# Two transformer blocks on one core: norm factors, gates, a weight's high part and the feed-forward squares put elsewhere

## The reference

```python
# block 1
h = rms_norm(x, g_mix_norm);  z = h @ w_in
y_a = mlstm_group(...)            # 4 heads, both directions:
#     h = rms_norm(h, g_out) per head;  return sigmoid(o) * h
y_b = mla_group(...)              # 4 heads of softmax attention
x = x + concatenate([y_a, y_b]) @ w_out
h = rms_norm(x, g_ffn_norm)
x = x + square(relu(h @ w_ff1)) @ w_ff2          # width 4096
# block 2
proj = rmsnorm(x, norm_mix_g) @ w_in
ry = retention(...)               # 4 heads
s = q k^T + bias;  p = softmax(s);  a = p[0] - lam * p[1];  dy = a @ v   # 4 heads, 4 query blocks
x = x + concatenate([ret_out, diff_out]) @ w_out
x = x + peer(rmsnorm(x, norm_ffn_g), ...)        # experts picked by product keys
return rmsnorm(x, final_norm_g)
# rms_norm(x) = x * rsqrt(mean(x*x) + 1e-6) * g
```

## Time and profile before

| | |
|---|---|
| median of 3 runs | 2349.71 us (2343.17, 2349.71, 2353.16) |
| the profiled execution's own time | 2352.68 us |
| its span | 2350.9 us |
| PE busy | 2288.5 us, 97% |
| DVE, POOL, ACT busy | 1347.7, 1178.3, 915.8 us |
| mean granted TensorE clock | 0.992 |

### The profile page before, as it was taken

One profiled execution on the slowest core, in us unless ns is written; L12 is line 12 of the kernel. 1 busy time (PEld: TensorE's weight loads), 2 busy tenths in 40 slices (PEclk: granted clock), 3 DMA queues, 4 the chain that ended last, 5 costly groups with the idle time before them and its releaser, 6 DMA issues.

```text
span 2350.9 us, 29628 instructions
## 1 busy us (share of the span) xinstructions
PE 2288.5 (97%) x11229; PEld 1143.2 (49%) x11429; DVE 1347.7 (57%) x2765; ACT 915.8 (39%) x1095; POOL 1178.3 (50%) x558
## 2 busy tenths in 40 slices
PE   8999999999999999999999999999999999999998
PEld 4556444444444564544566444444444444444443
DVE  3668474554425545898896555555555544555555
ACT  3233342333333443111687333344444334444432
POOL 1002346655543347410000676666666666888873
PEclk9999999999999999999999999999999999999999
DMA  6031358989752239834588886666666666776641
GB/s 220 0 108 37 142 168 247 259 238 262 226 156 72 72 126 261 223 117 157 206 323 311 286 244 201 197 197 192 192 194 189 193 170 176 200 203 172 173 113 45
DMA packets 404136, 427.16 MB, mean 182 GB/s; under 512 B 276258, under 2 KB 343078, under 8 KB 392500
## 3 DMA queue, kind: packets, MB, share of 16 engines
q1 hardware_dynamic: 397684, 414.05, 58.3%
q10 hardware_dynamic: 6336, 11.54, 1.3%
HBM read 286.06 MB, written 72.37 MB: 152 GB/s over the span
## 4 chain that ended last, share of the span: by engine, by line
PE 56%; DMA 2%; POOL 1%; ACT 1%; issue 1%; DVE 1%; SPq 1%; POOLq 0%; ACTq 0%; DVEq 0%
PE ps L1860 27%; PE ps L2168 23%; PE ps L2207 3%; DMA gate_matrix<-split 1%; PE ps L2184 1%; PE ps L2185 1%; DMA ring<-in_peer_v 1%; SPq L691 1%; PE ps L2133 1%; ACT split L1382 1%; POOL u_split L955 0%; POOL split L836 0%; PE ps L2073 0%; DMA arena<-u_split 0%; POOL u_split L841 0%
## 5 line engine op out<-in xcount | busy, mean ns | idle before, releaser
L1860 PE MATMUL ps<-split,arena 128*128 128x512 bf16 x3712 | 819.7, 380 | 5.8 <-DVE consts L2940 1.6
L1860 PEld LDWEIGHTS ps<-split,arena 128*128 128x128 bf16 x3792 | 371.1, 98 | 449.5 <-issue 4.3
L2168 PE MATMUL ps<-arena 128*128 128x512 bf16 x1886 | 415.7, 379 | 2.1 <-DMA arena<-u_split 0.3
L961 POOL TENSOR_TENSOR split<-ring,split 128x1024 bf16<-128x1024 f32 x140 | 299.3, 2146 | 76.4 <-ACT split L1417 76.4
L836 POOL TENSOR_TENSOR split<-ring,split 128x4096 bf16<-128x4096 f32 x26 | 207.2, 7971 | 197.1 <-ACT split L1189 194.7
L1860 PE MATMUL ps<-arena,split 128*128 128x512 bf16 x1316 | 296.8, 381 | 5.0 <-DVE arena L2640 2.0
L2168 PEld LDWEIGHTS ps<-arena 128*128 128x128 bf16 x1920 | 187.7, 98 | 227.2 <-DMA arena<-u_split 0.8
L955 POOL TENSOR_TENSOR u_split<-ring,u_split 128x1024 bf16<-128x1024 f32 x80 | 167.7, 2127 | 191.1 <-ACT u_split L1404 191.1
L947 POOL TENSOR_TENSOR split<-ring,split 128x1024 bf16<-128x1024 f32 x44 | 92.7, 2138 | 258.1 <-ACT split L1414 258.1
L1860 PEld LDWEIGHTS ps<-arena,split 128*128 128x128 bf16 x1344 | 142.9, 107 | 150.0 <-DVE arena L2640 6.1
L1417 ACT ACTIVATE split<-ring 128x1024 bf16<-128x1024 f32 x140 | 146.3, 1054 | 172.2 <-POOL ring L971 66.6
(11 more groups left out here) (357 smaller groups left out, 3125.1 us busy)
## 6 DMA issues: line engine op xcount, KB each, us to landing
ring<-in_peer_v SPq DMA_DIRECT2D x32, 2048.0 KB, 8.3
ring<-in_peer_u SPq DMA_DIRECT2D x20, 2048.0 KB, 12.0
ring<-in_w_ff SPq DMA_DIRECT2D x16, 2048.0 KB, 8.2
gate_matrix<-split SPq DMA_DIRECT2D x16, 2048.0 KB, 7.5
arena<-gate_matrix SPq DMA_DIRECT2D x32, 1024.0 KB, 6.8
arena<-in_peer_u SPq DMA_DIRECT2D x48, 512.0 KB, 4.8
turned_table<-u_split SPq DMA_DIRECT2D x48, 512.0 KB, 5.6
ring<-turned_table SPq DMA_DIRECT2D x12, 2048.0 KB, 9.1
```

The lines of the kernel that those rows point to most:

```text
L961: pool.tensor_tensor(part_place(i, 1), block, part_place(i, 0), ALU.subtract).then_inc(v_lo, 1)
L1860: mm = pe.matmul(dst, a(k), b(k), start=n == 0, stop=n == len(terms) - 1)
L2168: mm = pe.matmul(up_bank(j), a, b, start=n == 0, stop=n == len(terms) - 1)
```

## The change

It moves instructions of ACT, POOL and DVE, cuts two of ACT's into parts, and puts the feed-forward squares into PSUM, with the wait of PE that this needs. On POOL:

```diff
             mlstm_rms(0)
             mlstm_rms(1)
+            mlstm_rms(2)
             pool.wait_ge(w_hi, 1)
             ... (four first_low subtractions)
-            mlstm_rms(2)
             mlstm_rms(3)
@@
                 if s == 18:
                     inverse_rms(1, D, 33, 0)
+                    inverse_rms(1, D, 34, 1)
                 split_low(s, s % 4)
                 if s == 18:
-                    inverse_rms(1, D, 34, 1)
+                    inverse_rms(1, D, 35, 2)
                 for b in range(2):
                     pre_low(2 * (s - 3) + b, b)
-                    if s == 18 and b == 0:
-                        inverse_rms(1, D, 35, 2)
@@
             pre_late(SOON)
+            inverse_rms(1, D, 69, 0)
             split_low(27, 3)
-            inverse_rms(1, D, 69, 0)
             inverse_rms(1, D, 70, 1)
```

On ACT:

```diff
+                if t == 3:
+                    act.wait_ge(mm_out, 15)
+                    act.activation(o1[:, 0:3, :], o1[:, 0:3, :], ACT.Sigmoid).then_inc(o_sig, 1)
                 nope_rows(t)
             z_out(15)
             act.wait_ge(mm_out, 16)
-            act.activation(o1, o1, ACT.Sigmoid).then_inc(o_sig, 1)
+            act.activation(o1[:, 3, :], o1[:, 3, :], ACT.Sigmoid).then_inc(o_sig, 1)
@@
-            def out_high(c):
+            def out_high(c, part=slice(0, 4096), last=True):
                 act.wait_ge(ring_in[1 + c], arrived(1 + c, 1))
-                act.activation(split[:, c, 0, :], ring[:, 1 + c, :], ACT.Copy).then_inc(w_hi, 1)
+                step = act.activation(split[:, c, 0, part], ring[:, 1 + c, part], ACT.Copy)
+                if last:
+                    step.then_inc(w_hi, 1)
@@ for h in range(H):
                 attend_exp(4 * h + 1)
+                if h >= 2:
+                    out_high(0, slice(1024 * (2 * h - 3), 1024 * (2 * h - 2)), h == H - 1)
@@ (at the end of head h)
-                if h == 2:
-                    out_high(0)
+                if 1 <= h < H - 1:
+                    out_high(0, slice(2048 * (h - 1), 2048 * (h - 1) + 1024), False)
@@
             mix2_squares(0)
             split_high(18, 2, 5)
+            mix2_squares(1)
             pre_high(15, 0)
-            mix2_squares(1)
             pre_high(15, 1)
```

On PE and DVE (`hid` is gone from the memory plan, and DVE waits for `o_sig` 2 in place of 1):

```diff
                 for j in range(4):
-                    pe.wait_ge(ff_relu, 4 * g + max(j - 1, 0))
+                    pe.wait_ge(ff_lo, 4 * g + max(j - 1, 0))
@@ ff_square
-                    dve.tensor_tensor(hid[:, j % 2, :], relu[:, j % 2, :], relu[:, j % 2, :], ALU.mult).then_inc(ff_sq, 1)
+                    dve.scalar_tensor_tensor(bank(2 + j % 2), bank(2 + j % 2), 0.0, relu[:, j % 2, :], ALU.max, ALU.mult).then_inc(ff_sq, 1)
@@
-                    dve.tensor_tensor(hid_lo[:, par, j, :], hid[:, j % 2, :], hid_hi[:, par, j, :], ALU.subtract).then_inc(ff_lo, 1)
+                    dve.tensor_tensor(hid_lo[:, par, j, :], bank(2 + j % 2), hid_hi[:, par, j, :], ALU.subtract).then_inc(ff_lo, 1)
@@ for i in range(H * NT + 3):
+                if i == H * NT:
+                    mixed_probs(i - 1)
@@ (behind the copies)
                 if i == H * NT:
-                    mixed_probs(i - 1)
                     decayed_scores(0)
```

More of the change, by code:

```diff
@@ L242, in build @@
         relu = part(arena, 8192, 2, T)
-        hid = part(arena, 9216, 2, T)
         hid_hi = part(arena, 10240, 2, 4, T, dt=BF16)
@@ L2604, in _ @@
                 if h == 0:
-                    dve.wait_ge(o_sig, 1)
+                    dve.wait_ge(o_sig, 2)
             attend(H * NT)
```

## The result

| | before | changed |
|---|---|---|
| median, 15 runs each | 2348.46 us (2342.62 to 2353.16) | 2356.14 us (2353.05 to 2360.52) |
| ratio | | 1.0035, 95% interval 1.0029 to 1.0042 |
| profiled execution, its span | 2352.68, 2350.9 us | 2357.91, 2356.1 us |
| mean granted TensorE clock | 0.992 | 0.995 |

A forecast was written before the change was run, and what follows sets the result against it. PE, busy 97% of the span, was taken as the bound. Terms 21.4 - 4.9 - 0.7 - 0.85 - 1.05 = +13.9 us put the median at 2363.5 us (+0.59%); 80% range 2350 to 2373, the forecast's own 2358 to 2372.

The forecast's parts named there:

- Feed-forward, waits: Up products wait for the low part: +2.25 us at the start of group 1, +13.2 over six later groups.
- The part that it takes away: Feed-forward: DVE's square drops to 0.7 us and relu waits go; -3.0 us, 2.0 of it measured, 1.0 estimated.
- the nine us: Feed-forward: five losses of PE clock, 1.8 us each, behind seven new waits; +9.0 us, bounds 0 and 20.
- Gates: First head: PE's wait falls from 2.29 to 0.35 us and the lower clock behind it goes; -4.9 us.
- Weight split in four: Last head: PE's 1.59 us wait goes, but POOL's subtractions hold DVE; -0.7 us, bounds 0 and -3.4.
- Norms: Ahead of block 2 and experts: DVE's scaling stays held by POOL, waits shrink 0.5 and 0.35; -0.85 us.
- Probabilities: Last block: mixing moves into DVE's idle time, so PE's wait shortens; -1.05 us, bounds 0 and -1.75.
- the clock falls little: Feed-forward rival: new waits come, but with none to two clock losses; 2354.5 to 2358 us, chance 0.25.
- DVE not held: Norms rival: POOL doesn't hold DVE's row scaling, so both waits go; +5 us, 2354.7, chance 0.06.
- the sigmoid in place: First head rival: sigmoid's parts wait for the last copy, leaving a 2 us wait; +19, 2369 us, chance 0.04.
- the low part never late: Feed-forward rival: the load lands 2.6 us or more earlier, so the waits go; -6.5, 2343 us, chance 0.08.

The follow-up runs named there:

- e3: The changed kernel with ACT's first square in groups 1 to 7 moved ahead of the second table conversion (`pre_high`); 2340.58 us, 0.9969 of before.
- e4: e3 with tile 0, in group 1 and later, waiting for the low part of three tiles ago instead of two; 2338.46 us, 0.9959 of before.
- e1: The kernel before with only the four feed-forward lines of the change; 2364.76 us, 1.0067 of before.
- e6: e4 with POOL subtracting each quarter of the first output chunk as soon as ACT has made it; 2333.45 us, 0.9942 of before.
- e12: e6 unchanged, run again in a later batch; 2333.56 us, 0.9938 of before.
- e2: The changed kernel with its four feed-forward lines as before; 2341.66 us, 0.9966 of before.
- e5: e4 with the high part of the first output chunk copied whole again behind head 2; 2335.5 us in one execution.
- e7: e4 with POOL's long subtractions ahead of block 2 and of the experts in four instructions of 1024 columns each; 2339.32 us, 0.9966 of before.
- e9: The kernel before, unchanged, executed once more for a second trace; 2348.07 us.

## Why the prediction came out as it did

**Feed-forward, waits: right, place and size.** The seven waits sum to 15.2 us where 2.25 + 13.2 = 15.45 were worked out, and e3 and e4 show both mechanisms apart: six end with ACT's order, the seventh with the wait's own count. The part that it takes away holds too: DVE's square takes 0.70 us, the relu waits are gone, and e4's 2.9 us shorter stretch answers to the forecast 3.0.

**Feed-forward, "the nine us" of clock: wrong, and the largest error.** The step that failed is "with seven new waits of 2.0 to 2.6 us I take five losses". There were two, in the changed kernel and in e1, of 1.5 to 1.6 us each as far as the products behind the waits show it, instead of five of 1.8: about 3 us, not 9. In all the stretch got 16.2 us longer in the trace, forecast 21.4; the terms measured here (15.2 + 3.1, less 2.0 of relu waits and the estimated 1.0) make 15.3, and 0.9 stay unassigned. No length of a wait settles it. The rule of the Trainium skill weighed in the prediction ("TensorE: Matmul & The Clock Gate", "Why this matters for your kernels": no drop for gaps up to about 3 us) fits five of the seven waits and not the other two, nor the 1.59 us wait in front of the last head before. e6 and e12 differ at a wait of one and the same length. Why the clock falls behind one wait and not behind another stays open. What could be carried from the profile of before was a share of waits that cost clock, not a length from which they do; three kinds of it in one profile were too few to set this share at five sevenths.

**Gates: right.** PE's first wait is 0.32 us (0.35 forecast) and ends at 158.43, ACT's table load and sigmoid stand at 142.55 in its idle time, and no lower clock follows. From the first scores of the first head to those of the second the changed kernel is 4.9 us shorter (4.9 forecast), and so are e2, e3 and e4.

**Weight split in four: the mechanism right, the size and with it the sign wrong.** Forecast was -0.7 between bounds of 0 and -3.4; the stretch got 1.9 us longer. The prediction named DVE held by POOL until 240.5 (234.9 was measured, the high part being complete at 226.4 and not at 232), but its bound took "all given back" as the worst. The changed kernel shows more than all given back: the wait ahead of the last head (1.59) goes, the one of 1.2 behind the last scores becomes one of 3.29, and the clock is at the lower level behind it for 6.8 us, where it was for 3.4 behind the wait of 1.59. In this stretch e5 is shorter than e4 by 2.3 us and e6 by 3.2. The bound should have reached above zero.

**Norms: right in what holds them.** DVE's scaling is 5.03 us long beside POOL (4 to 8 forecast), and PE's wait fell from 3.7 to 3.14, 0.55 for the forecast 0.5. The Trainium skill, "SBUF — State Buffer", section "Who interferes with whom", names `tensor_scalar`, which this scaling is, among the DVE operations that can contend with GpSimd in a two-port mode, where the first to issue keeps the ports for its whole instruction. The traces agree: 5.03 us beside an instruction of 4096 columns, 1.29 beside a quarter in e7. The other 2 us by which this stretch got shorter go with the clock: before has it at 0.5 for 10.2 us there, behind two waits, the changed kernel for 3.4, behind one. Ahead of the experts the forecast was read from an execution whose table load came late: the wait of 2.51 us to be shortened isn't in the second execution of before (e9), nor in e1, which has the old order, and it goes with the lateness of the load in either order (see e9). What the moved root brings at that place is not told apart from nothing.

**Probabilities: right.** The wait fell from 1.8 to 0.7, -1.1 for -1.05.

**The sum.** Without the feed-forward part the change is worth -6.9 us by e2's median; forecast were -7.5. The feed-forward part by e1 is +16.2, forecast +21.4. The error of the sum, 6.2 us of median, is in the main the clock term: 9.0 forecast, 3.1 measured. In the profiled execution, where the two are 8.7 us apart (13.9 and 5.2), the other differences are the last head (2.6 worse than forecast), clock and a late load of before's own execution (2.0 ahead of block 2 and 3.5 ahead of the experts) and the start (0.6). The rival "the clock falls little" (2354.5 to 2358, up to two losses) is what happened; it stood at 0.25 against 0.57 for the forecast. With it came "within 0.5%", which stood at 0.37, and not "slower by over 0.5%", which stood at 0.58. The rivals on DVE not held and on the sigmoid in place are refuted by the 5.03 us and the 0.32 us; the one on the low part never late by the 15.2.

Of the versions measured e6 is the one to keep: the changed kernel with the square ahead of the table conversion, the exact wait and the subtraction in step with the copy. It is 0.58% faster than before (0.62% in its second batch).

## What to carry to other kernels

When a product starts to wait for a longer chain, walk that chain along each engine's list: the slack is eaten not by the operations of the chain but by whoever stands ahead of one of them and waits for a DMA. Moving one 0.6 us instruction ahead of such a wait turned a loss of 0.35% into a gain of 0.3%, and this was the difference between a bad idea and a fair one. And where a copy is cut into parts, the one who reads it has to be cut too, or the work that was spread out comes back in one block at the worst place.

## What the runs showed of the hardware

- The clock behind a wait isn't settled by the wait's length. In the feed-forward waits of 1.25 to 2.49 us kept 2.4 GHz, others of 2.25, 2.31, 2.48 and 2.70 were followed by 1.2 GHz; the one of 3.13 us ahead of block 2 went both ways in two executions of one kernel, on two chips. In the feed-forward a drop cost 1.5 to 1.6 us.
- A DVE operation as small as 128x8 is held as well: 1.98 us instead of 0.17, until POOL's 128x1024 subtraction beside it had ended.
- Two executions of one kernel differed by up to 2.5 us in when a table row's load was used (8.8 and 11.3 us after issue), and by 4.0 us in the stretch ahead of the experts. PE's wait there was 0 at 8.7 to 9.0 us, 0.24 at 9.2, 1.32 at 10.1, 2.10 at 11.1 and 2.51 at 11.3. One profile is not enough for terms of this size there.
